# The gated blocks of four SwiGLU layers turned by VectorE's square transposes and DMA instead of TensorE

## What is computed

```python
def swiglu(x, w_in, w_out):
    g, u = jnp.split(x @ w_in, 2, axis=-1)
    return (jax.nn.silu(g) * u) @ w_out      # w_in 1024 x 5632, w_out 2816 x 1024
```

## Time and profile before

| | us |
|---|---|
| median of 3 runs | 973.5 (972.28 to 973.59) |
| profiled execution | 969.86 |
| its span | 967.7 |

### The profile page before, as it was taken

The page is one execution under the profiler, slowest core; times in us unless marked ns, Lnnn a source line. Parts: engine busy times, 40 slices in busy tenths (PEclk is TensorE's granted clock), DMA queues, the critical chain, the costliest instruction groups (busy, mean ns, idle before and its releaser), DMA issues.

```text
span 967.7 us, 15102 instructions
## 1 busy us (share of the span) xinstructions
PE 955.9 (99%) x6110; PEld 790.2 (82%) x6110; DVE 597.8 (62%) x744; ACT 499.8 (52%) x711; POOL 189.5 (20%) x235
## 2 busy tenths in 40 slices
PE   9999999999999999999999999999999999999997
PEld 7888888788788888888888888888888888888886
DVE  5565779889765554656555555555557555656544
ACT  7554544576555454545544454554458454545441
POOL 4899999800000000000000000000060000000000
PEclk9999999999999999999999999999999999999999
DMA  9766555520455655565566666656651366555551
GB/s 347 269 184 197 181 174 174 175 69 5 142 187 193 194 178 194 184 208 183 166 198 196 193 177 196 191 177 195 188 182 45 111 198 193 186 187 192 179 169 43
DMA packets 47557, 169.35 MB, mean 175 GB/s; under 512 B 5505, under 2 KB 5505, under 8 KB 47489
## 3 DMA queue, kind: packets, MB, share of 16 engines
q1 hardware_dynamic: 47056, 167.79, 54.5%
q10 hardware_dynamic: 432, 0.61, 0.2%
HBM read 167.33 MB, written 1.05 MB: 174 GB/s over the span
## 4 chain that ended last, share of the span: by engine, by line
PE 88%; DVE 8%; issue 2%; ACT 1%; DMA 1%; SPq 0%; POOLq 0%; POOL 0%; DVEq 0%; ACTq 0%
PE ps L1252 85%; DVE w_lo L931 2%; PE ps L1257 2%; DVE scan L1158 1%; DVE tmp L1087 1%; PE ps L1284 1%; DMA raw<-in_in 1%; DVE rot_b L1165 1%; DVE rot_a L1145 1%; DVE rot_b L1147 1%; ACT w_hi L652 0%; DVE rot_in L1154 0%; DVE states L1172 0%; PE ps L1297 0%; ACT pr L881 0%
## 5 line engine op out<-in xcount | busy, mean ns | idle before, releaser
L931 DVE TENSOR_TENSOR w_lo<-raw,w_hi 128x1024 fp32r<-128x1024 f32 x311 | 399.7, 1289 | 307.0 <-ACT w_hi L652 305.7
L652 ACT ACTIVATE w_hi<-raw 128x1024 fp32r<-128x1024 f32 x311 | 328.4, 1059 | 305.9 <-PE ps L1252 303.2
L1252 PE MATMUL ps<-w_hi,x_hi 128*128 128x512 f32 x896 | 352.4, 393 | 0.9 <-DVE w_lo L931 0.6
L1252 PE MATMUL ps<-w_hi,x_lo 128*128 128x512 f32 x896 | 349.3, 390 | 0.0
L1252 PE MATMUL ps<-w_lo,x_hi 128*128 128x512 f32 x896 | 349.2, 390 | 0.0
L1252 PEld LDWEIGHTS ps<-w_hi,x_hi 128*128 128x128 f32 x896 | 168.4, 188 | 37.2 <-DVE w_lo L931 1.4
L1252 PEld LDWEIGHTS ps<-w_hi,x_lo 128*128 128x128 f32 x896 | 168.3, 188 | 35.2
L1252 PEld LDWEIGHTS ps<-w_lo,x_hi 128*128 128x128 f32 x896 | 168.5, 188 | 34.0
L1252 PE MATMUL ps<-w_hi,hid_hi 128*128 128x512 f32 x352 | 138.1, 392 | 1.0 <-DVE w_lo L931 1.0
L1252 PE MATMUL ps<-w_lo,hid_hi 128*128 128x512 f32 x352 | 137.2, 390 | 0.0
L1252 PE MATMUL ps<-w_hi,hid_lo 128*128 128x512 f32 x352 | 137.2, 390 | 0.0
(11 more groups left out here) (151 smaller groups left out, 599.6 us busy)
## 6 DMA issues: line engine op xcount, KB each, us to landing
raw<-in_in SPq DMA_DIRECT2D x175, 512.0 KB, 4.3
raw<-in_out SPq DMA_DIRECT2D x88, 512.0 KB, 3.4
raw<-in_glu SPq DMA_DIRECT2D x16, 512.0 KB, 4.3
raw<-in_k SPq DMA_DIRECT2D x8, 512.0 KB, 4.4
raw<-in_v SPq DMA_DIRECT2D x8, 512.0 KB, 4.1
raw<-in_q SPq DMA_DIRECT2D x8, 512.0 KB, 4.4
raw<-in_o SPq DMA_DIRECT2D x8, 512.0 KB, 4.0
xt<-in_xt SPq DMA_DIRECT2D x4, 256.0 KB, 5.6
```

What stands on the lines that cost most here:

```text
L652: act.activation(w_hi[:, gu % WS, :], raw[:, gu % RAW, :], ACT.Copy)\
L931: dve.tensor_tensor(w_lo[:, gu % WS, :], raw[:, gu % RAW, :], w_hi[:, gu % WS, :].bitcast(F32), ALU.subtract)\
L1252: return pe.matmul(o, w, x, start=start, stop=stop, skip_group_check=True)
```

## The change

TensorE no longer turns the gated blocks. VectorE writes the gated block so that its 512 columns are ordered by the 128-wide half of the block, then by token half, and transposes every 32 x 32 square of it in place (`dve.transpose`, 128 x 512). A pair of blocks is held in `prod` or `prod2` in turn. When both blocks of a pair are done, SP issues sixteen transfers from SBUF to SBUF that bring each row and column of squares to its place in `hid_lo`: source partitions 32q to 32q+31, destination partitions 32c to 32c+31, for each partition 8 pieces of 32 floats (4 for the last block of a phase, which is alone). Four of them stand behind each of four weight loads, from the load of the ninth unit behind the pair on. ScalarE then copies the high half from `hid_lo` in SBUF, and VectorE subtracts it in place. The places of the high and low halves move: the pair that ended one block ago is taken at the units 1 and 2 (high) and 2 and 3 (low) of a block with an odd number.

```diff
--- before.py
+++ after.py
@@ -17,6 +17,8 @@
 
 P = 128
 HP = P // 2
+Q = 32
+QS = P // Q
 TOK = 256
 TT = TOK // P
 D = 1024
@@ -65,8 +67,8 @@
 
 X_OF = {2: [(2, 1)], 4: [(3, 0), (4, 1)], 8: [(5, 0)], 10: [(6, 0)]}
 FINAL = 12
-BATCH = 4
-BATCHES = (0, 4, 8)
+MOVE_BEHIND = 8
+MOVED = 16 * QS * QS
 TABLE_AT = (1, 3, 5, 7, 9, 11, 12, 13, 14, 15, 16, 17)
 
 
@@ -108,36 +110,33 @@
     return [(phases[p.n - 1], phases[p.n - 1].blocks - 1, j)] if chained else []
 
 
...
+def pair_end(p, b):
+
+    return min(b // 2 * 2 + 1, p.blocks - 1)
+
+
+def pair_number(p, b):
+
+    return p.hid0 // p.blocks * ((p.blocks + 1) // 2) + b // 2
+
+
...
+def high_behind(p, phases, b, j):
+
+    if p.name == "in" and b >= 3 and b % 2 and j in (1, 2):
+        return [(p, b - 4 + j)]
+    if p.name == "out" and b == 0 and j in (1, 2, 6):
         f = phases[p.n - 1]
+        return [(f, f.blocks - 4 + j if j < 3 else f.blocks - 1)]
+    return []
+
+
+def low_behind(p, phases, b, j):
+
+    if p.name == "in" and b >= 3 and b % 2 and j in (2, 3):
+        return [(p, b - 5 + j)]
+    if p.name == "out" and b == 0 and j in (2, 3, 7):
         f = phases[p.n - 1]
+        return [(f, f.blocks - 5 + j if j < 4 else f.blocks - 1)]
     return []
@@ -257,16 +256,27 @@
         def w_columns(d):
             return w2[:, :, :, PPT * d:PPT * d + PPT, :].rearrange("p r s g j -> p (r s) g j")
 
-        def prod_of(b):
-            i = b % BATCH
-            return prod[:, i] if i < 2 else prod2[:, i - 2]
+        def pair_of(k):
+            return prod if k % 2 == 0 else prod2
+
+        def tile_of(p, b, q):
+            return prod_of(p, b).rearrange("p i (t x) -> p t i x", x=P)[:, q]
+
+        def pieces(p, b, n, q, c):
+
+            return pair_of(pair_number(p, b))[Q * q:Q * q + Q, 0:n]\
+                .rearrange("p b t (a c x) -> p c (b t a) x", a=2, x=Q)[:, c]
+
+        def places(b, n, q, c):
+
+            return hid_lo[Q * c:Q * c + Q, 2 * b:2 * (b + n), :].bitcast(F32)\
+                .rearrange("p i (t q x) -> p q (i t) x", t=TT, x=Q)[:, q]
+
         def halves(a):
             return a.rearrange("p (b h x) -> p b h x", h=2, x=HP)
-
-        def turned_block(b):
-            at, col = KT + b % BATCH // 2 * 2, b % 2 * HB
-            return ps[:, at:at + 2, col:col + HB].rearrange("p h (b x) -> p b h x", x=HP)
 
         def z_place(d):
             i = d % Z_SLOTS
...
+            def move_hidden(p, b, q):
+                k, n = pair_number(p, b), pair_end(p, b) + 1 - b
+                sp.wait_ge(hid_squares, p.hid0 + b + n)
+                for c in range(QS):
+                    sp.dma_start(places(b, n, q, c), pieces(p, b, n, q, c)).then_inc(hid_moved[k % 2], 16)
+
+            moves = {p.unit0 + (pair_end(p, b) + 1) * p.upb + MOVE_BEHIND + q: (p, b, q)
+                     for p in phases if p.name == "in" for b in range(0, p.blocks, 2) for q in range(QS)}
+
             for c in range(DT // 2):
                 sp.dma_start(xt[:, 2 * c:2 * c + 2, :], io["xt"][:, 2 * c:2 * c + 2, :])\
                   .then_inc(x_in[c], 16)
@@ -427,6 +447,8 @@
                              io[name].rearrange("p (r x) -> p r x", r=2)).then_inc(s5_in, 16)
             for gu in range(10, len(units)):
                 load(gu)
+                if gu in moves:
+                    move_hidden(*moves[gu])
             for q in range(TT):
                 for ready, cols in ((left_ready, slice(0, NB)), (right_ready, slice(NB, D))):
                     sp.wait_ge(ready, q + 1)
@@ -676,9 +698,10 @@
                                        ACT.Sigmoid).then_inc(act_ready, 1)
 
             def high_hidden(p, b):
-                act.wait_ge(hid_turned, p.hid0 + min(b // BATCH * BATCH + BATCH, p.blocks))
-                act.activation(halves(hid_hi[:, 2 * b:2 * b + 2, :].rearrange("p f x -> p (f x)")),
-                               turned_block(b), ACT.Copy).then_inc(hid_hi_done, 1)
+                k = pair_number(p, b)
+                act.wait_ge(hid_moved[k % 2], MOVED * (k // 2 + 1))
+                act.activation(hid_hi[:, 2 * b:2 * b + 2, :], hid_lo[:, 2 * b:2 * b + 2, :].bitcast(F32),
+                               ACT.Copy).then_inc(hid_hi_done, 1)
 
             def squares(p, b, w):
                 for q in range(TT):
@@ -963,12 +986,11 @@
                     dve.wait_ge(act_ready, p.acts0 + TT * b + q + 1)
                     gb = p.block0 + b
                     if p.name == "in":
-                        if b >= BATCH:
-                            dve.wait_ge(hid_turned, p.hid0 + b - BATCH + 1)
-                        elif p.hid0:
-                            dve.wait_ge(hid_turned, p.hid0)
-                        dve.scalar_tensor_tensor(prod_of(b)[:, q, :], ps[:, bank(gb, q), HB:NB],
-                                                 rs[:, q:q + 1], act_out[:, q, :],
+                        k = pair_number(p, b)
+                        if k >= 2:
+                            dve.wait_ge(hid_moved[k % 2], MOVED * (k // 2))
+                        dve.scalar_tensor_tensor(tile_of(p, b, q), halved(ps[:, bank(gb, q), HB:NB]),
+                                                 rs[:, q:q + 1], halved(act_out[:, q, :]),
                                                  ALU.mult, ALU.mult).then_inc(drained, 1)
                     else:
                         cols = slice(HB * b, HB * b + HB)
@@ -976,13 +998,16 @@
                                                act_out[:, q, :], ALU.mult))
                         dve.tensor_tensor(h[:, q, cols], h[:, q, cols], prod[:, 0, q, :], ALU.add)\
                            .then_inc(drained, 1)
+                if p.name == "in":
+                    dve.wait_ge(drained, p.drained0 + TT * (b + 1))
+                    whole = prod_of(p, b).rearrange("p t x -> p (t x)")
+                    dve.transpose(whole, whole).then_inc(hid_squares, 1)
 
             def low_hidden(p, b):
-                dve.wait_ge(hid_hi_done, p.hid0 + min(b // 2 * 2 + 2, p.blocks))
-                dve.tensor_tensor(halves(hid_lo[:, 2 * b:2 * b + 2, :].rearrange("p f x -> p (f x)")),
-                                  turned_block(b),
-                                  halves(hid_hi[:, 2 * b:2 * b + 2, :].rearrange("p f x -> p (f x)")
-                                         .bitcast(F32)), ALU.subtract).then_inc(hid_ready, 1)
+                dve.wait_ge(hid_hi_done, p.hid0 + b + 1)
+                part = hid_lo[:, 2 * b:2 * b + 2, :]
+                dve.tensor_tensor(part, part.bitcast(F32), hid_hi[:, 2 * b:2 * b + 2, :].bitcast(F32),
+                                  ALU.subtract).then_inc(hid_ready, 1)
 
             def residual(p, b):
                 for q in range(TT):
@@ -1257,21 +1282,6 @@
                     last = pe.transpose(ps[:, at + r, col:col + HP], src[rows, :], ident[rows, rows])
                 return last
 
-            def turn_hidden(f, batch):
-                if not batch:
-                    return
-                pe.wait_ge(drained, f.drained0 + TT * (batch[-1] + 1))
-                if f.hid0 + batch[0]:
-                    pe.wait_ge(hid_ready, f.hid0 + batch[0])
-                if f.n == 7 and batch[0] == 0:
-                    pe.wait_ge(kq_ready, 4)
-                for b in batch:
-                    for i in range(2):
-                        for q in range(TT):
-                            last = turn(KT + b % BATCH // 2 * 2, b % 2 * HB + (2 * i + q) * HP,
-                                        prod_of(b)[:, q, i * P:i * P + P])
-                    last.then_inc(hid_turned, 1)
-
             def turn_h(p, c):
 
                 t = turned[p.n, c]
@@ -1361,8 +1371,6 @@
                         unit(p, b, j)
                         for done in follow_ups(p, phases, b, j, chained):
                             after(*done)
-                        if j == 1:
-                            turn_hidden(*batch_behind(p, phases, b))
                         if n == 9 and b == 1 and j >= 2:
                             scores(j - 2)
```

26 lines of the change are left out of this document (5 added, 21 removed).

## The result

The changed kernel takes 974.58 us (median of 20 runs, 971.44 to 977.20), the kernel before on the same chip 972.06 (20 runs). The ratio is 1.0025 with a 95% interval of 1.0017 to 1.0034: slower by 2.5 us. I had forecast 5.5 us less; the direction was wrong. In the profiled executions the difference is 4.6 us (974.42 against 969.86), since the profiled one of before lies 2.2 us under its median.

The account below looks back on a forecast made before the run. The prediction took TensorE's matmul stream as the bound, and GpSimd's end up to 178 us. Turns −11.5 plus GpSimd's delay 6.0 gave −5.5 us, from 973.5 to 968.0; range 962.0 to 970.2 within this case.

Parts of the forecast that it names:

- TensorE's turns go: Phases 3/4, 7/8 and 11/12: removing the turns gains 11.5 us; the 3.8 us of phases 0 and 1 count as nothing.
- GpSimd's end decides: Up to 178 us the end of GpSimd's S5 coefficient run sets the time; TensorE has no slack against it.
- Low halves against GpSimd: Phases 0 and 1: low halves with two SBUF operands hinder GpSimd; with one table operation, 6.0 us of delay.
- TensorE doesn't wait: Every pair: the moved squares give weights in time for TensorE, with 2.8 us left.
- The sum T + 1.0, + 1.8, + 16.0: After T, the end of a pair's second block: last gating product ends, transpose ends, last transfer lands.
- T + 18.8: Latest landing of a pair's transfers before TensorE must wait, counted from the end of the pair's second block.
- The size of lateness, steady phases: Steady pairs: the last transfer lands at T + 16.0 and ScalarE stands 3 to 4 us, without TensorE waiting.
- The transposes: VectorE's 44 square transposes take 0.68 us each, 0.7 us a block in the steady phases, and cost nothing.
- A: Rival: transfers come late in all 20 full pairs; at 1.0 us per transfer 48 us lost, 1016; 16 in 100.
- SP's time per transfer: Transfer issue: taken as 0.65 us; TensorE waits from 0.84, and above that the prediction would be wrong.
- B: Rival: the transposes shut GpSimd out as well, another 5.5 us, no change at 973.5; 12 in 100.
- C: Rival: the low halves cost GpSimd nothing, so the gain is 11.5 us alone, 962.0; 8 in 100.

Follow-up runs that it names:

- e1: The changed kernel with the high and low halves taken two units later in every phase: 964.82 us, ratio 0.9933.
- e2: The changed kernel with one plain transfer per pair in place of sixteen, values not brought to their places: 964.16 us, ratio 0.9926.
- e4: The changed kernel without VectorE's square transposes, squares moved unturned: 971.64 us, ratio 0.9999.
- e7: The hybrid (phase 0 as in the kernel before, the three other SwiGLUs as changed) with their halves two units later: 958.03 us, ratio 0.9874.
- e10: The changed kernel with all high and low halves one unit later: 964.64 us, ratio 0.9940.
- e12: The changed kernel with halves two units later and GpSimd's large S5 coefficient operations replaced by fills that read nothing: 953.52 us, ratio 0.9821.
- e11: The kernel before with GpSimd's large S5 coefficient operations replaced by fills that read nothing: 967.96 us, ratio 0.9970.
- e5: The kernel before, turns on TensorE kept, with the low half reading two SBUF operands: 974.22 us, ratio 1.0038.
- e3: The changed kernel with GpSimd's large S5 coefficient operations replaced by fills that read nothing: 960.88 us, ratio 0.9888.
- e6: The hybrid: phase 0 turned by TensorE as in the kernel before, the three other SwiGLUs as changed: 961.78 us, ratio 0.9905.

## Why the prediction was wrong, by its own steps

The median was to fall to 968.0 and is 974.58; the 973.5 from which it was counted was a median of three, and that of twenty is 972.06. In the profiled executions the change was to be −5.5 us and is +4.7 in the span. The 10.2 us between them are, by the table: 7.3 in phases 0 and 1 (13.3 late at the mixer instead of 6.0), 1.6 between there and phase 2, and 1.3 in the phases 3 to 12 (10.2 gained instead of 11.5).

- **TensorE's turns go: right.** −11.5 was said for the phases 3 to 12. Six kernels in which the moved squares come earlier or are taken later (e1, e2, e4, e7, e10, e12) take 663.7 or 663.8 against 675.5, 11.8 less; the changed kernel itself 10.2 less. The 3.8 us of phases 0 and 1 are worth nothing where GpSimd's end decides, as was said (in e1 the mixer starts 16.0 us behind it, as before), and are there without it: e12 starts the mixer 4.2 us before e11.
- **Low halves against GpSimd: right in mechanism, hidden by something worse.** 6.0 was said; 4.2 in e5 and 5.8 in e2. In the changed kernel the term did not show, since a VectorE that stands still collides less: GpSimd ended earlier.
- **"TensorE doesn't wait": this is the step that failed.** The sum T + 1.0, + 1.8, + 16.0, with 2.8 us left against T + 18.8, was worked out with steady rows of phase 3 alone and then used for all 20 pairs. In phases 0 and 1 TensorE waits: 12.1 us in eight times, and 5.1 us of lower clock behind them. A subtraction takes 1.99 us there instead of 1.23, so VectorE has no time free to make up ScalarE's wait, and its next products and transposes are late in turn: the wait grew from 6.0 us at 70 to 8.8 at 95 and 9.3 at 150. I had the needed fact, and wrote it down: "In 139.5 to 180 VectorE is full". I dismissed it, since that stretch ended at GpSimd's last coefficient. So it did; but an engine that is full at one bound is at the next one as soon as work or waiting is added. That is the 7.3 us at the mixer. Taking the halves two units later (e1) gives 10.0 us back there, which shows the lateness as the cause. How much of it is owed to the full VectorE is less sure: without GpSimd's reads lateness still costs 4.7 us (e3 against e12).
- **The size of lateness, steady phases: undersized.** In phase 3 the second silu, T, starts at 369.97, and the pair's high half at 387.72 (rows below), T + 17.8 instead of T + 16.0. The largest term is the one that I had from the kernel before: the last product ends at T + 2.5 and the transpose at T + 3.2, not at T + 1.0 and T + 1.8, since VectorE has just stood 5.04 us for ScalarE and takes three subtractions and two low halves first. The loop in which a late square delays the next is thus in the steady phases as well. SP needs 0.61 us a transfer (0.65 was said), but 0.60 for a load that stands behind transfers where I had 0.37, and the first transfer starts at T + 3.3. ScalarE waits 5 us rather than 3 to 4, and 1.0 us is left of the 2.8. This lateness costs the phases 3 to 12 of the changed kernel 1.5 us (665.3 against 663.8), and 3.2 in e6. ScalarE's timeline:

```profile
365.36 0.63 ACT L703 ACTIVATE hid_hi<-hid_lo 128x512 fp32r<-128x512 f32 x1 [4.85 <-DMA hid_lo<-prod]
...
369.97 0.47 ACT L694 ACTIVATE act_out<-ps,rs 128x256 f32<-128x256 f32 x1 [0.25 <-PE ps L1277]
...
387.72 0.63 ACT L703 ACTIVATE hid_hi<-hid_lo 128x512 fp32r<-128x512 f32 x1 [5.45 <-DMA hid_lo<-prod]
```

  and VectorE's around the same T:

```profile
366.97 1.23 DVE L954 TENSOR_TENSOR w_lo<-raw,w_hi 128x1024 fp32r<-128x1024 f32 x1 [5.04 <-ACT w_hi L674]
...
371.59 0.87 DVE L992 SCALAR_TENSOR_TENSOR prod<-ps,rs,act_out 128x256 f32<-128x256 f32 x2
372.50 0.71 DVE L1004 STREAM_TRANSPOSE prod<-prod 128x512 f32<-128x512 f32 x1
```

- **The transposes** take 0.71 us each, 0.68 was said. "Cost nothing" holds in the steady phases; in phases 0 and 1 they are part of a full engine, and e4 has them at some 3 us with the delay they bring.
- **The rivals.** A was the right one, the transfers come late, and I had it decide by SP's time per transfer (0.84 us, and slower than before from 0.87, where 5.5 us over 20 pairs and 15 transfers give 0.86), which stayed far below at 0.61. What decided here is when VectorE finishes the square and what it has free to make up a wait. B is refuted by e2: with all transposes in it, GpSimd ends 5.8 us later, what the low halves explain, and not 11.5. C is refuted by e5.
- **What stays open:** from the mixer's start to the last turn of phase 2 the kernels differ by up to 2.7 us (97.5 us before, 99.1 changed, 100.2 in e2), without an order that a theory here would give.

## What to carry to other kernels

A slack is a property of a stage and not of a kernel: before a step with a new wait is called hidden, the waiting engine's whole load over one period is added up once for each stage, with that stage's own durations, and the wait must fit into what is left. When a transfer takes the place of a computation, move its consumers as far back in program order as their deadline allows, since an in-order engine that waits for it holds up everything behind it; here one or two units of 2.7 us turned a loss of 2.5 us into a gain of 6 to 7. Two units were already more than the deadline of one low half allowed (the stop of 3.7 us in e1), and bought no more than one. And where one stage can't take a change, leave it out there: the hybrid with late halves gains 12 us.
